# Attention in a transformer stack: values as stationary weights, an outcome laid out by features, probabilities divided first, and one fused mask-and-maximum

## The reference

```python
def mixer_a(h, w_qkv, rel_bias, w_o):          # 16 heads of 64
    q, k, v = jnp.split(h @ w_qkv, 3, axis=-1)
    s = jnp.einsum('bqhd,bkhd->bhqk', qc, kb).astype(jnp.float32) * scale + bias
    s = jnp.where(valid, s, NEG_INF)
    p = jax.nn.softmax(s, axis=-1).astype(vb.dtype)
    o = jnp.einsum('bhqk,bkhd->bqhd', p, vb)
    return o @ w_o
```

## Time and profile before

| | |
|---|---|
| median of three runs | 2672.31 us (2668.22 to 2673.62) |
| profiled execution | 2668.04 us |
| its span | 2666.2 us |
| mean granted clock of TensorE | 0.986 of 2.4 GHz |
| PE busy | 2595.0 us, 97% |
| DVE busy | 1695.7 us, 64% |
| ACT busy | 1317.7 us, 49% |
| DMA, mean | 173 GB/s |

### The profile page before, as it was taken

One profiled execution on the slowest core, in us unless ns is written; L12 is line 12 of the kernel. 1 busy time (PEld: TensorE's weight loads), 2 busy tenths in 40 slices (PEclk: granted clock), 3 DMA queues, 4 the chain that ended last, 5 costly groups with the idle time before them and its releaser, 6 DMA issues.

```text
span 2666.2 us, 43254 instructions
## 1 busy us (share of the span) xinstructions
PE 2595.0 (97%) x18557; PEld 2415.7 (91%) x18557; DVE 1695.7 (64%) x2204; ACT 1317.7 (49%) x1932; POOL 156.7 (6%) x228
## 2 busy tenths in 40 slices
PE   7989999999999999999999999999899999999999
PEld 7979889898998989989988998998789899898997
DVE  5768658685665656647656765666766566565663
ACT  6746457564443545444454544444454454354542
POOL 2110011000000000000010000002010000000000
PEclk9999999999999989999999999999989999999999
DMA  7266542575666527657664766666347566562763
GB/s 209 87 163 185 189 143 93 148 188 187 177 196 203 188 76 211 190 173 198 190 207 140 202 188 182 191 187 200 128 126 195 191 177 198 186 204 93 200 188 126
DMA packets 568280, 460.19 MB, mean 173 GB/s; under 512 B 12314, under 2 KB 529258, under 8 KB 568090
## 3 DMA queue, kind: packets, MB, share of 16 engines
q1 hardware_dynamic: 562643, 441.88, 56.3%
q0 software_dynamic: 4656, 15.30, 1.7%
q10 hardware_dynamic: 791, 0.25, 0.0%
HBM read 456.30 MB, written 1.10 MB: 172 GB/s over the span
## 4 chain that ended last, share of the span: by engine, by line
PE 90%; DVE 5%; ACT 3%; DMA 1%; issue 1%; SPq 0%; POOL 0%; DVEq 0%; POOLq 0%; ACTq 0%
PE ps L793 28%; PE ps L724 16%; PE ps L726 16%; PE ps L725 16%; PE ps L678 3%; PE ps L680 3%; PE ps L679 3%; PE ps L620 1%; DVE wlo L1668 1%; ACT h_hi L1181 1%; DMA raw<-in_w_in 1%; DVE h_lo L1729 1%; ACT whi L1181 1%; ACT prob L1181 1%; PE ps L884 0%
## 5 line engine op out<-in xcount | busy, mean ns | idle before, releaser
L1668 DVE TENSOR_TENSOR wlo<-raw,whi 128x2048 fp32r<-128x2048 f32 (+1 forms) x420 | 958.8, 2285 | 509.1 <-ACT whi L1181 508.4
L1181 ACT ACTIVATE whi<-raw 128x2048 fp32r<-128x2048 f32 (+1 forms) x420 | 802.5, 1915 | 800.1 <-DMA raw<-in_ff_w_in 422.7
L724 PE MATMUL ps<-h_hi,whi 128*128 128x256 f32 x3648 | 1027.0, 282 | 3.3 <-DVE h_lo L1729 3.3
L725 PE MATMUL ps<-h_lo,whi 128*128 128x256 f32 x3648 | 1023.1, 280 | 0.0
L726 PE MATMUL ps<-h_hi,wlo 128*128 128x256 f32 x3648 | 1022.9, 280 | 0.0
L724 PEld LDWEIGHTS ps<-h_hi,whi 128*128 128x128 f32 x3648 | 688.0, 189 | 9.0 <-issue 9.0
L726 PEld LDWEIGHTS ps<-h_hi,wlo 128*128 128x128 f32 x3648 | 689.1, 189 | 0.0
L725 PEld LDWEIGHTS ps<-h_lo,whi 128*128 128x128 f32 x3648 | 687.7, 189 | 0.0
L793 PE MATMUL ps<-whi,hid_lo 128*128 128x512 f32 x880 | 296.1, 396 | 0.0
L793 PE MATMUL ps<-whi,hid_hi 128*128 128x512 f32 x880 | 295.0, 394 | 0.0
L793 PE MATMUL ps<-wlo,hid_hi 128*128 128x512 f32 x880 | 294.4, 394 | 0.0
(11 more groups left out here) (294 smaller groups left out, 2204.5 us busy)
## 6 DMA issues: line engine op xcount, KB each, us to landing
raw<-in_ff_w_in SPq DMA_DIRECT2D x176, 1024.0 KB, 6.1
raw<-in_ff_w_out SPq DMA_DIRECT2D x88, 1024.0 KB, 4.9
raw<-in_ffn_w_in SPq DMA_DIRECT2D x44, 1024.0 KB, 6.1
raw<-in_a_w_qkv SPq DMA_DIRECT2D x24, 1024.0 KB, 5.2
raw<-in_ffn_w_out SPq DMA_DIRECT2D x22, 1024.0 KB, 4.9
raw<-in_w_in SPq DMA_DIRECT2D x20, 1024.0 KB, 5.3
raw<-in_c_w_qkv SPq DMA_DIRECT2D x12, 1024.0 KB, 5.3
raw<-in_w_out SPq DMA_DIRECT2D x8, 1024.0 KB, 5.0
```

What stands on the lines that cost most here:

```text
L724: e.matmul(out, hi, m.h_hi[:, k, :], start=(k == 0), stop=False)
L725: e.matmul(out, hi, m.h_lo[:, k, :], start=False, stop=False)
L1181: return self.nc.scalar.activation(*a, **k)
L1668: self.e.tensor_tensor(chunk_view(m.wlo[:, slot, :], c), chunk_view(m.raw[:, slot, :], c), chunk_view(m.whi[:, slot, :], c).bitcast(F32), ...
```

## The change

It does five things.

- `values` for kind a: the values of a head are the stationary operand (128 x 64), the turned probabilities stream (256 columns, then 128 into the second half). The two heads write partitions 0 to 63 and 64 to 127 of bank 3, which puts them in column halves of the array. The outcome stands features by tokens. Kind c is as before.
- `keep_out` for kind a is a plain copy into `out_t`, a view of `xn` by pairs. `pairs_hi` (ScalarE) and `pairs_lo` (VectorE) make `h_hi` and `h_lo` from it, for two pairs at a time: 0 and 1 of these groups at chunk 12, 2 at chunk 13, 3 where `turn` was. The 16 transposes, their copies and subtractions are gone.
- `weigh` for kind a multiplies the probabilities by the reciprocals in place, four instructions, and `turn_probs` waits for that (`shares`) instead of the exponentials.
- `first_tile`: token tile 0 of the first output chunk (12 matmuls) is issued behind the transposes of pair 7, ahead of pair 7's values. Tile 1 follows; its half 1 uses bank 3 and waits for the last eviction. `wait_block` goes by groups of two pairs.
- `mask` for both kinds is four `tensor_tensor_reduce`: the negated sum goes out, and its minimum is the accumulator. `exps` reads with scale -1 and waits for `masked`; `maxed` is left to the first stack, and its count there is put right.

```diff
+PAIRS_AT = {12: (0, 1), 13: (2,)}
...
     def turn(self, ready):
+        if ready == "out_kept":
+            return
...
+    def first_tile(self, what):
+        self.c0 += 12
+        self.begin_out(what)
+        self.wait_block(0, 0)
+        self.block(self.c0, 2 * self.order[0], 0, range(2), True, False)
+        self.c0 -= 12
...
         for b in range(n):
             for t in range(TT):
-                self.wait_block(b, t)
-                self.block(self.c0 + b, 2 * order[b], t, range(2), b == 0, False)
+                if self.what == "a_o" and b == 0:
+                    if t == 0:
+                        continue
+                    self.block(self.c0, 2 * order[0], 1, (0,), True, False)
+                    self.e.wait_ge(self.s.out_kept, self.p0)
+                    self.block(self.c0, 2 * order[0], 1, (1,), True, False)
...
+            heads = [(out[64 * h:64 * h + 64, :], m.prob_t[:, b % 2, h, :], h) for h in range(2)]
+            for to, pt, h in heads:
+                e.matmul(to, v(b, h, 0), pt[:, 0:SEQ], start=True, stop=True)
+            for to, pt, h in heads:
+                ins = e.matmul(to[:, P:SEQ], v(b, h, 1), pt[:, SEQ:SEQ + P], start=False, stop=True, skip_group_check=True)
...
+    def pairs_hi(self, g):
+        m, s = self.m, self.s
+        if g == 0:
+            self.e.wait_ge(s.chunk_done, self.c0 + 12)
+        self.e.wait_ge(s.out_kept, self.p0 + 2 * g + 2)
+        self.act(m.h_hi[:, 2 * g:2 * g + 2, :], m.out_t[:, 2 * g:2 * g + 2, :], ACT.Copy).then_inc(s.hi_pairs, 1)
...
+    def pairs_lo(self, g):
+        e, m, s = self.e, self.m, self.s
+        e.wait_ge(s.hi_pairs, self.a0 // 2 + g + 1)
+        e.tensor_tensor(m.h_lo[:, 2 * g:2 * g + 2, :], m.out_t[:, 2 * g:2 * g + 2, :], m.h_hi[:, 2 * g:2 * g + 2, :].bitcast(F32),
+                        ALU.subtract).then_inc(s.features, 1)
...
-            e.tensor_tensor(out[:, 0:P], sc[:, 0:P], tab[:, 0:P][:, ::-1], ALU.add)
-            ins = e.tensor_tensor(out[:, P:], sc[:, P:], tab[:, ::-1], ALU.add)
+            for t, cols, src in ((0, slice(0, P), tab[:, 0:P]), (1, slice(P, 3 * P), tab)):
+                ins = e.tensor_tensor_reduce(out[:, cols], sc[:, cols], src[:, ::-1], -1.0, 3e38, ALU.add, ALU.min,
+                                             m.negmax[:, par, h, t:t + 1])
         ins.then_inc(s.masked, 1)
-        self.at(s.masked, self.p0 - 4 * self.rounds["mixers"] + b + 1)
-        e.tensor_reduce(m.negmax[:, par, :, 0:1], m.prob[:, par, :, 0:P], AX, ALU.max, negate=True)
-        e.tensor_reduce(m.negmax[:, par, :, 1:2], m.prob[:, par, :, P:], AX, ALU.max, negate=True).then_inc(s.maxed, 1)
...
+        self.at(s.recips, self.p0 + b + 1)
+        if kind == "a":
+            for h in range(2):
+                for t, cols in ((0, slice(0, P)), (1, slice(P, 3 * P))):
+                    ins = e.tensor_scalar(m.prob[:, par, h, cols], m.prob[:, par, h, cols], m.rsum[:, par, 2 * h + t:2 * h + t + 1],
+                                          None, ALU.mult)
+            ins.then_inc(s.shares, 1)
             return
...
+            e.tensor_copy(m.out_t[:, b, :], m.ps[:, m.out_bank[kind], 0:SEQ]).then_inc(s.out_kept, 1)
```

More of the change, by code:

```diff
@@ L181, in __init__ @@
         self.out_kept = new("out_kept")
+        self.shares = new("shares")
+        self.hi_pairs = new("hi_pairs")
         self.bias_ready = new("bias_ready")
@@ L375, in attend @@
         self.m0 += 8 if kind == "c" else 0
+        self.a0 += 8 if kind == "a" else 0
         self.advance(12)
     m0 = 0
+    a0 = 0
     def advance(self, n, banks=True):
@@ L1305, in turn @@
         m, s = self.m, self.s
+        if ready == "out_kept":
+            self.p0 -= 8
+            self.pairs_hi(3)
+            self.p0 += 8
+            return
         r = self.round("turn")
@@ L1351, in attend_pairs @@
                 self.exps(kind, b)
+        if kind == "a" and c in (12, 13):
+            for g in PAIRS_AT[c]:
+                self.pairs_hi(g)
+    def pairs_hi(self, g):
[4 more added lines that the diff above has]
+        self.act(m.h_hi[:, 2 * g:2 * g + 2, :], m.out_t[:, 2 * g:2 * g + 2, :], ACT.Copy).then_inc(s.hi_pairs, 1)
     def square_out(self, b):
@@ L1440, in exps @@
         m, s, par = self.m, self.s, b % 2
-        self.at(s.maxed, self.p0 + b + 1)
+        self.at(s.masked, self.p0 - 4 * self.rounds["mixers"] + b + 1)
         for h in range(2):
@@ L1837, in turn @@
     def turn(self, ready):
+        if ready == "out_kept":
+            self.a0 -= 8
+            self.pairs_lo(3)
+            self.a0 += 8
+            return
         e, m, s = self.e, self.m, self.s
@@ L1898, in attend_pairs @@
                 self.mask(kind, b)
+        if kind == "a" and c in (12, 13):
+            for g in PAIRS_AT[c]:
+                self.pairs_lo(g)
+    def pairs_lo(self, g):
[3 more added lines that the diff above has]
+                        ALU.subtract).then_inc(s.features, 1)
     def hidden(self, kind, l):
```

55 lines of the change are left out of this document (27 added, 28 removed).

## The result

The changed kernel takes 2647.32 us (median of four runs, 2645.50 to 2650.00), the kernel before beside it 2671.91 (2668.22 to 2673.62). The ratio is 0.991, its 95% interval 0.9897 to 0.9922: a gain of 24.6 us (20.8 to 27.5), where 11 were forecast.

What follows compares the result with a forecast made beforehand. TensorE's matmul queue, busy 97%, was taken as the bound. Layer a's tails gave 9.6 + 5.7 - 4.5 (clock) = 10.8 us, layer c 0: 2657 us profiled, 2661 for the median, range 2654 to 2671.

Steps and rivals of the forecast that it cites:

- The mask: Four fused instructions on VectorE replace four additions and two reductions: some 2.0 us instead of 2.20, a gain of 0.2.
- Layer c: Its last two masks: 0 to 0.8 us lost by later scores, 0.2 us gained each; booked as 0.
- rival B: Fused mask bound by columns, 3.5 us each, VectorE becomes the bound: 15 us lost against 11, time 2676; chance 0.08.
- The tails of layer a: Uncovered chain behind the last weight chunk: the 24 output matmuls end 9.6 us earlier in the first layer, 5.7 in the second.
- the clock: TensorE's idle time in layer a's tails brings half clock: 3 us lost in the first layer, 1.5 in the second.
- the values: Values as weights in layer a, heads in column halves: 0.95 us a pair instead of 1.28, a gain of 0.3.
- The wait of `weigh(7)`: In layer a's tail on VectorE, weigh(7) stands 2.6 us behind two pairs_lo steps that nobody needs yet.
- The covered parts: Between layer a's weight chunks only TensorE's time counts; VectorE's row scaling, 1.2 us a pair, is hidden there.
- From the profiled run to the median: Whole kernel: 2657 us for the profiled run, raised by the 4.3 us it lay below the median, to 2661.
- A: Column halves run in sequence: layer a's values take 1.6 us instead of 0.95; gain 2 us, time 2670; chance 0.17.
- D: Layer a's first tile isn't early, as weigh(7) waits; only 16 transposes less, 3 us a layer, 2666; chance 0.08.
- C: Both layer a tails stay at 1.2 GHz: another 6 to 7 us go, 2668 at worst; part of the forecast's spread.

Runs made afterwards that it cites:

- e5: The changed kernel with seven more fused instructions and a plain addition behind layer c's own two fused ones, into unused places; ran once, 2648.2 us.
- e3: The changed kernel with three more fused instructions behind each mask, so that a mask takes 2.02 us; 2660.95 us, ratio 0.9964.
- e12_changed_again: The changed kernel with no edit, run again in a later set; 2645.92 us, ratio 0.9898.
- e11: The changed kernel with both heads' values of kind a in one column half and two copies in keep_out (outcome not the reference's); 2652.9 us, ratio 0.9928.
- e4: The changed kernel with weigh(7) issued ahead of pairs_lo(0) and pairs_lo(1) on VectorE; 2640.64 us, ratio 0.9885.
- e10: The changed kernel with five fused and five plain instructions added at chunk 2 of layer c, beside and behind GpSimd's last work; ran once, 2645.36 us.

## Why the prediction was wrong in size

**The mask: the step that failed.** "If that is a fixed part: ... some 2.0 us with the last read", and "both ends stay for the range", 2.0 to 3.5. It is 1.20 with the last read, and VectorE is free again after 1.12. The price came from the two rows of 64 columns, which waited for GpSimd and took twice their time and more (0.34 against 0.15, e5). Three things in the trace of before spoke against it. GpSimd's instructions beside the two rows stand in it. The read of the accumulator (1858.10) starts together with the next fused instruction (1858.10), so it needn't be a part of its own. And the plain additions of the same four sizes, 1.08 us in the earlier trace rows, are the price of a fused instruction that costs nothing extra. That belonged in the range as its lower end, and the prediction looked only for reasons why the form should be dearer than a plain one.

The Trainium skill, "Vector Engine (DVE) Microarchitecture Reference", Points that are easy to get wrong, has such a reason: two SBUF sources that aren't bf16 halve the throughput of the `S2S2D2_STT` form. Whether it means this fused form too, it doesn't say. If it did, 256 columns from two fp32 tensors in SBUF should take twice those with one in PSUM; the trace doesn't agree, both take 0.35 us (e5).

**Layer c: 0 booked, 6.0 us measured.** It follows from the same price. The prediction saw that TensorE waits for VectorE there, priced it at the last two masks alone (0 to 0.8 us lost, 0.2 gained), and used it for all eight only as a loss (rival B, 1.3 us a mask). The same wait turns a mask that is 1.0 us cheaper into a gain: seven masks' worth were collected at the chunks, 6.9 us, and 6.0 are left at the end. At a mask of 2.0 us "0" is right (e3: 0.1).

**The tails of layer a: right, but for the clock.** With the steps in and out the values give 0.35 us a pair for 0.3, and mask (7) comes 1.7 us earlier in the layer for 1.5. The wait of `weigh(7)` was there, 2.8 us for 2.6. The 24 matmuls end 17.1 us behind mask (7), within the 13 to 18 given; the sum had 14.95 and 3 for the clock. In the second layer they end 16.4 behind it (2419.54 to 2435.93), for 14.95 and 1.5. That these sums meet is in part luck: 3 and 1.5 us for the clock were booked by how long TensorE is idle, and idle time alone doesn't tell it. In `e12_changed_again` TensorE is idle for 1.47, 0.95 and 2.06 us in both tails, as in the changed kernel's first, and the clock never falls there. In the kernel before 2.5 and 0.95 us idle go with 13.6 us at half clock in one layer and with 3.4 in the other. The prediction's "2.5 + 0.9 us after which it stood at 1.2 GHz" is also misread: it stood there from 964.0, ahead of the second of the two (969.17). Without weight in the sum, the first output matmul of before starts at 975.81; 976.15 is the end of the last transpose's record. The covered parts cost nothing, as said: TensorE is busy for all of the time from 905 to 953.5 us.

**From the profiled run to the median.** The sum was made against the profiled execution (2657) and then moved up by 4.3 us, the distance of before. The changed kernel's profiled execution took 2650.0, 7 us below that sum, of which layer c is 6. But its median lies 2.7 below its own profiled run and not 4.3 above: another 7 us. The runs' granted clocks are 0.985 in the middle for the kernel before (24 executions over all sets) and 0.989 for the changed kernel, where the two profiled ones have 0.986 and 0.987. By an estimate from these: 2 x (1 - 0.985) of 2670 us are 80 us at half clock, against 58 at 0.989, and up to half of the difference, 11 us, is lost time; in the profiled pair (75 and 69 us) it is 3. So by this estimate the clock gives the typical run more than the profiled pair shows: it was booked as a loss of 4.5 us, and on balance it would be a gain. No run separates it from the rest. What can be seen is how far two runs of one program differ by it. The windows of the two layers a in `e12_changed_again` (columns as in the earlier trace rows):

```profile
870.00:1010.00 140.00, 135.07 (x1045) 122.53 (x1044) 93.39 (x196) 77.06 (x143) 10.09 (x18) 1.00 0.53 162
2330.00:2475.00 145.00, 140.06 (x1084) 127.39 (x1083) 97.99 (x201) 80.68 (x149) 10.51 (x19) 1.00 0.54 164
```

and in the changed kernel's profiled run:

```profile
870.00:1010.00 140.00, 135.06 (x1021) 121.98 (x1020) 91.48 (x193) 75.48 (x142) 10.28 (x18) 0.98 0.52 159
2330.00:2475.00 145.00, 140.37 (x1061) 126.69 (x1060) 96.79 (x206) 79.19 (x149) 10.79 (x19) 0.98 0.52 159
```

The same program, once with and once without the half clock in its tails: 1.00 against 0.98. The span is 2644.6 against 2648.2 us, and by the splits the first of them gains some 10 and 6.5 us in the two layers a, for 7.5 and 4.4.

**The rivals.** A fell: side by side, 0.80 us, and e11 shows what it would have cost, up to 7 us (9 forecast). B had the right place and the wrong sign. D's wait is real but the tile does come early; with both tiles behind the values the prediction's own terms give about 15.85 instead of 14.95, so 0.9 us a layer for the tile. The rows agree (0.95), and the medians say 2.7 or 6.0 us for both layers, by the run set beside it. C was part of the spread; by the estimate above the miss on the median is partly the clock's.

## What to carry to other kernels

Before a row becomes a price, look at what ran beside it on the other engines and find a second row of the same engine and size: a fused elementwise instruction is priced first as the plain one of its width, and a dearer figure is the upper end. Where one engine waits for another, the same wait prices a cheaper step as a gain and a dearer one as a loss, so book both. On an engine that works in order, put what the end of the chain waits for ahead of what nobody needs yet; a wait removed in an uncovered tail also gave clock back (in e4 2.1 us by the wait and 2.7 by the clock).

## What the hardware showed that was not expected

- The accumulator of `tensor_tensor_reduce` costs no time on VectorE but for the last read, 0.08 us: 128 columns 0.21, 256 columns 0.34 us from start to start, as plain additions, from SBUF and PSUM alike.
- VectorE and GpSimd take turns where a VectorE instruction with both inputs in SBUF meets a GpSimd `tensor_scalar` from SBUF to SBUF: the later one waits for the end of the other's instruction. 64 columns take 0.33 to 0.37 us instead of 0.15, fused or plain (27 times in fourteen traces), and a GpSimd instruction of 0.41 us takes 2.3 to 2.5 us beside a weight split (41 times). With an input in PSUM no wait showed (two in e10).
- Two fp32 streams over all 128 rows in the two column halves run side by side, whichever order they are issued in: 0.80 us a pair against 1.44 in one half. The step from full-width matmuls into them takes 0.21 us instead of 0.12.
- With the same three idle stretches in its tails (1.47, 0.95 and 2.06 us) one program ran once at full clock and once with 6.8 us at half clock.
- The spread between runs of one program goes with the clock. Over 24 executions of the kernel before the mean time is 2674.8 us at a mean granted clock of 0.983 (4 runs), 2671.9 at 0.984 (7), 2671.1 at 0.985 (7), 2670.1 at 0.986 (4) and 2668.7 at 0.987 (2).
